# Near bias of the second softmax of three heads added by the vector engine, outputs of the first attention scaled by the scalar engine

## The chip, the cores and the metric

One core of a Trainium2 chip. The metric is device time in microseconds of one execution, lower is better.

## The reference

One layer of a streaming encoder on x of 1024 frames by 1024 channels: an RMSNorm, one projection, two mixers side by side, gates, an output projection, a residual and a last RMSNorm. The first mixer is a differential attention with 4 heads; the second is an attention with 8 heads over 256 keys that an indexer selects for each query. The part that matters here is the first one:

```
s = einsum('bqhd,bkhd->bhqk', qb, k) * scale + bias     # T5 bias by relative position
s = where(allowed, s, -inf)                             # key chunk <= query chunk, chunks of 64
p = softmax(q1, k1) - lam * softmax(q2, k2)
ao = einsum('bhqk,bkhd->bqhd', p, v)
```

Its output is normed, scaled and multiplied by a SiLU gate.

## The kernel before

The kernel is written engine by engine, with semaphores that each engine waits on by hand; every engine runs its instructions in the order written. The program has these stages: norm and transposes of x, the indexer's scores, the first projection (groups A), the **first attention** (252 to 381 us), the second projection (groups B), the second attention, the output projection.

Top-k selection runs on the vector engine (`select`: rounds of MAX8 and MATCH_REPLACE8): one part before the first attention, the larger part right after it and beside the second projection. It ends with the mask for the second attention, whose PSUM moves on the scalar engine wait for `mask_made`.

The first attention has 32 steps: 4 heads (blocks 0 to 3) times 8 tiles of 128 queries, in the order 2, 4, 6, 7, 5, 3, 1, 0. Tile i sees 128(i+1) keys, so the widths of a block are 384, 640, 896, 1024, 768, 512, 256, 128. Each step s has two softmaxes (m = 0, 1), and the engines work on it in a pipeline:

- TensorE, `scores(ph, s, m)`: q times k in float32r in two passes, then for the nearest 256 columns the bias. The bias is split in a high and a low part and added by two matmuls with the identity (L1171, L1172). A 640-wide tile has its band in two banks, so it needs two such pairs. Later come `turn` (transposes of the combined probabilities), `fill` (a slice of the next projection) and `weigh` (the product with V, L1208), which run one step behind.
- Vector engine, step s: `finishA(s-2)` (L1517) scales the output of step s-2 out of PSUM by 1/sum; `far_min(0, s+1, 0)` (L1453), the maximum (a minimum of negated scores) of the next first softmax; `invert` (L1482), `factor` (L1498) and `combine` (L1507), which subtracts the second softmax from the first; `far_min(0, s+1, 1)`.
- Scalar engine, step s: `turned(s-1)` (L872) copies the turned probabilities to SBUF, `exp(s+1, 0)` (L861), `finish(s-2)` squares the scaled output and sums it, `exp(s+1, 1)`.
- GpSimd gates the scaled output (L647), once for each step, and between those splits q and k of the next head into float32r parts (`split_q`, `split_k`). The split for head b+1 starts with step 8b-2. Two DMA copies of the split keys follow (`copy_keys`), for which the first scores of that head wait.

In the second attention the vector engine already adds the bias itself: `far_min` on the far columns and `soften` (L1474), a custom instruction that adds the bias to the scores in PSUM and takes the minimum in one pass; it is followed by a read of its accumulator.

Of the kernel before, what the change touches and what calls it, by code (L numbers as in the profile page):

```python
# [22 lines left out]
P = 128  # L23
CHUNK = 64
# [17 lines left out]
MASKED = 1e30  # L42
# [30 lines left out]
def build(nc, x, norm_w, w_in, w_out, lambda_q1, lambda_k1, lambda_q2, lambda_k2, subln_w,  # L73
# [61 lines left out]
    biasA_hi, _ = place("biasA_hi", [P, A_HEADS, BAND], f32r)  # L135
    biasA_lo, _ = place("biasA_lo", [P, A_HEADS, BAND], f32r, at=bias_at)
    ident_r, _ = place("ident_r", [P, P], f32r)
    k1_low = [place(f"k1_zero_low{b}", [P, SEQ], f32r)[0] for b in range(2)]
# [46 lines left out]
    with ctx:  # L185
# [7 lines left out]
        def bank(n):  # L193
            return psum[:, n * HALF:(n + 1) * HALF]
# [143 lines left out]
        def quads_through(ph, s):  # L338
            return quads[ph, s][-1][0] + 1
# [58 lines left out]
        def same_slot(n):  # L398
# [3 lines left out]
            return max(k for k in range(n) if k % SW == n % SW and k not in FILLS)  # L402

        def units_before(ph, b):

            return 2 * (ph * STEPS + b * TILES)
# [7 lines left out]
        def _(sp):  # L414
# [52 lines left out]

            def load_bias(h):
                sp.dma_start(bias[:, h, :],
                             bass.AP(scratch, h * RELS + P - 1, [[nh * RELS - 1, P], [1, BAND]])  # L470
                             ).then_inc(bias_loaded, 16)
# [9 lines left out]
            for h in range(A_HEADS):  # L481
                load_bias(h)
            for n in range(DB + SW, Q0 - 2):
                load_chunk(n)
# [221 lines left out]
        def _(act):  # L706
# [168 lines left out]
            def finish(s):  # L875

                if s >= 1:
                    act.wait_ge(o_squared, s)
                act.wait_ge(o_moved, s + 1)
                act.activation(sq_junk[:, :], o_tmp[:, s % 4, :], ACT.Square,  # L880
                               accum_out=ssA[:, s:s + 1]).then_inc(o_squared, 1)
# [3 lines left out]
            for s in range(STEPS + 2):  # L885
                qs = quads[0, s - 1] if 1 <= s <= STEPS else []
                turned(0, qs)
                if s + 1 < STEPS:
                    exp(0, s + 1, 0)
                if s >= 2:  # L890
                    finish(s - 2)
                if s >= 1 and s % TILES == 0:
                    move_fill(s // TILES - 1)
                if s + 1 < STEPS:
                    exp(0, s + 1, 1)
                if s == 13:
                    high(Q0 + 2)
                elif s == 17:
                    high(Q0 + 3)
                elif s == STEPS - 1:  # L900
                    high(Q0 + 4)
# [43 lines left out]
        def _(pe):  # L945
# [193 lines left out]
            def scores(ph, s, m):  # L1139
# [22 lines left out]
                for c in range(0, length, HALF):  # L1162
# [3 lines left out]
                    near = max(c, length - BAND)  # L1166
                    banded = (masked or ph == 0) and near < c + w
                    ins = pe.matmul(o, q[:, qt], low[:, c:c + w], start=False, stop=not banded)  # L1168
# [106 lines left out]
        def _(dve):  # L1275
# [144 lines left out]

            dve.wait_ge(bias_loaded, 16 * A_HEADS)
            dve.memset(bias[0:CHUNK, 0:A_HEADS, BAND - CHUNK:BAND], MASKED).then_inc(bias_masked, 1)


# [21 lines left out]
            def far_min(ph, s, m):  # L1446
# [4 lines left out]
                dve.wait_ge(s_ready, u + 1)  # L1451
                if ph == 0:
                    dve.tensor_reduce(negmax[:, u % 4:u % 4 + 1], score_of(u, 0, P * (i + 1)), AX.X, ALU.min  # L1453
# [8 lines left out]
            def soften(ph, s, m):  # L1462
# [7 lines left out]
                if u in far_done:  # L1470
                    dve.wait_ge(dve_own, far_done[u])
                    least = farmin[:, u % 4:u % 4 + 1]
                o = score_of(u, length - w, length)
                dve.tensor_tensor_reduce(out=o, in0=o, in1=bias[:, h, BAND - w:BAND], scale=1.0,  # L1474
                                         scalar=least, op0=ALU.add, op1=ALU.min,
                                         accum_out=negmax[:, u % 4:u % 4 + 1]).then_inc(max_ready, 1)

            def invert(ph, s):

                c = 2 * s % 8  # L1480
                dve.wait_ge(exp_done, 2 * (ph * STEPS + s) + 2)
                inverted[ph, s] = later(dve.reciprocal(rinv[:, c:c + 2], rsum[:, c:c + 2]))  # L1482
# [27 lines left out]

            def finishA(s):

                dve.wait_ge(pv_done, quads_through(0, s))
                if s >= 4:
                    dve.wait_ge(o_gated, s - 3)
                    dve.wait_ge(o_squared, s - 3)
                dve.tensor_scalar(o_tmp[:, s % 4, :], bank(O_BANK)[:, 0:P],  # L1517
                                  rinv[:, 2 * s % 8:2 * s % 8 + 1], None, ALU.mult).then_inc(o_moved, 1)

            ROUNDS = TOPK // 8  # L1520
# [5 lines left out]
            far_min(0, 0, 0)  # L1526
            far_min(0, 0, 1)
            for s in range(STEPS):
                if s >= 2:
                    finishA(s - 2)  # L1530
                if s + 1 < STEPS:
                    far_min(0, s + 1, 0)
                invert(0, s)
                factor(s)
                combine(s)
                if s + 1 < STEPS:
                    far_min(0, s + 1, 1)
            finishA(STEPS - 2)
            finishA(STEPS - 1)
            select(1, SEL0 + 1)  # L1540
# [5 lines left out]
            inverse_root(rA, ssA, rstdA, iw[:, 0:STEPS])  # L1546
            dve.wait_ge(bias_loaded, 16 * nh)
            link(dve.memset(bias[0:CHUNK, A_HEADS:nh, BAND - CHUNK:BAND], MASKED))
# [104 lines left out]
```

## Time and profile before

| what | value |
|---|---|
| median of 3 runs | 789.06 us (788.75 to 790.1) |
| profiled execution | 789.29 us, its span 787.4 us |
| PE busy | 753.8 us (96%) |
| PEld busy | 631.1 us (80%) |
| DVE busy | 613.3 us (78%) |
| ACT busy | 304.6 us (39%) |
| POOL busy | 318.8 us (40%) |
| granted TensorE clock | 0.997 |

PE is TensorE, DVE the vector engine, ACT the scalar engine, POOL is GpSimd. The durations of matmuls overlap, since they are pipelined: the step from one start to the next tells what one costs. The same holds to a smaller degree for the vector and the scalar engine, where a start lies up to 0.1 us ahead of the end before it when nothing is waited for.

### The profile page before, as it was taken

How to read it: one execution, taken by the hardware profiler on the slowest of the kernel's cores; microseconds unless marked ns; L12 is line 12 of the kernel's file. 1: busy time of each engine (PE TensorE's matmuls, PEld its weight loads, DVE VectorE, ACT ScalarE, POOL GpSimd, SP SyncE). 2: the span in 40 equal slices, each digit the busy share in tenths (PEclk: the TensorE clock that was granted, in tenths of full speed). 3: DMA queues.
4: the chain of work that ended last, by engine and by line, in shares of the span. 5: the costliest groups of instructions: out<-in, count | busy, mean ns of one | idle time of the engine just before them, and what ended most of it. 6: DMA issues, size and time to landing. Idle time of an engine off the chain costs nothing.

```text
span 787.4 us, 11733 instructions
## 1 busy us (share of the span) xinstructions
PE 753.8 (96%) x4161; PEld 631.1 (80%) x4161; DVE 613.3 (78%) x1300; ACT 304.6 (39%) x677; POOL 318.8 (40%) x383
## 2 busy tenths in 40 slices
PE   3999999999999999999999999998999999899996
PEld 2765888888887888889888888887888888788885
DVE  3738999999999979978899999994767667524343
ACT  5437222130315566757421313007545455422221
POOL 5320121223538857751355554457996400300000
PEclk9999999999999999999999999999999999999999
DMA  7242111111210011040121111300311100222231
GB/s 261 73 122 67 41 41 53 46 49 54 68 54 0 1 41 29 14 122 1 41 63 45 54 43 51 81 1 27 109 54 55 28 2 1 70 79 79 81 107 53
DMA packets 24560, 44.54 MB, mean 57 GB/s; under 512 B 3076, under 2 KB 9912, under 8 KB 24376
## 3 DMA queue, kind: packets, MB, share of 16 engines
q1 hardware_dynamic: 24504, 43.81, 18.6%
q8 instruction: 33, 0.54, 0.3%
q14 instruction: 23, 0.19, 0.1%
HBM read 35.40 MB, written 6.57 MB: 53 GB/s over the span
## 4 chain that ended last, share of the span: by engine, by line
PE 70%; DVE 23%; ACT 3%; issue 2%; DMA 1%; POOL 1%; SPq 0%; DVEq 0%; ACTq 0%; POOLq 0%
PE psum L1103 22%; PE psum L1208 11%; PE psum L1269 11%; DVE score L1434 9%; DVE top L1429 9%; PE psum L1190 5%; PE psum L1165 4%; PE psum L1003 4%; PE psum L1168 4%; PE psum L1031 3%; PE psum L1047 2%; ACT probsT_B L872 1%; DVE small L1453 1%; PE psum L1176 1%; DVE probs L1507 1%
## 5 line engine op out<-in xcount | busy, mean ns | idle before, releaser
L560 POOL TENSOR_TENSOR w_lo<-w_raw,w_hi 128x512 fp32r<-128x512 f32 x60 | 77.8, 1300 | 219.3 <-ACT w_hi L715 218.9
L1434 DVE MATCH_REPLACE8 score<-top,score 128x768 f32<-128x768 f32 (+5 forms) x176 | 157.3, 907 | 0.0
L1429 DVE MAX8 top<-score 128x8 f32<-128x768 f32 (+5 forms) x176 | 148.2, 909 | 1.0
L715 ACT ACTIVATE w_hi<-w_raw 128x512 fp32r<-128x512 f32 x60 | 37.7, 630 | 215.0 <-PE psum L1103 209.2
L861 ACT ACTIVATE probs<-psum,small 128x384 f32<-128x384 f32 (+7 forms) x128 | 94.8, 741 | 49.0 <-DVE small L1453 32.2
L1103 PE MATMUL psum<-w_hi,big_hi 128*128 128x512 f32 x256 | 99.6, 389 | 0.0
L1103 PE MATMUL psum<-w_lo,big_hi 128*128 128x512 f32 x256 | 99.6, 389 | 0.0
L1103 PE MATMUL psum<-w_hi,big_lo 128*128 128x512 f32 x256 | 99.6, 389 | 0.0
L1208 PE MATMUL psum<-v,probsT_B 128*128 128x64 f32 x576 | 74.8, 274 | 3.7 <-ACT probsT_B L872 2.6
L1208 PEld LDWEIGHTS psum<-v,probsT_B 128*128 128x128 f32 x576 | 70.4, 192 | 8.0 <-ACT probsT_B L872 3.6
L1103 PE MATMUL psum<-big_hi,w_hi 128*128 128x512 f32 x192 | 74.9, 390 | 0.0
L1103 PE MATMUL psum<-big_lo,w_hi 128*128 128x512 f32 x192 | 74.7, 389 | 0.0
L1103 PE MATMUL psum<-big_hi,w_lo 128*128 128x512 f32 x192 | 74.7, 389 | 0.0
L1190 PE MATMUL psum<-ident,probs 128*128 128x128 f32 x432 | 63.8, 274 | 1.6 <-issue 1.3
L1103 PEld LDWEIGHTS psum<-w_hi,big_hi 128*128 128x128 f32 x256 | 48.1, 188 | 10.1
L1103 PEld LDWEIGHTS psum<-w_lo,big_hi 128*128 128x128 f32 x256 | 48.1, 188 | 10.0
L1453 DVE TENSOR_REDUCE small<-psum 128x1 f32<-128x384 f32 (+7 forms) x64 | 48.0, 751 | 10.4 <-PE psum L1172 9.6
L1103 PEld LDWEIGHTS psum<-w_hi,big_lo 128*128 128x128 f32 x256 | 48.1, 188 | 9.8
L1190 PEld LDWEIGHTS psum<-ident,probs 128*128 128x128 f32 x432 | 49.7, 145 | 2.3 <-issue 1.5
L1269 PE MATMUL psum<-big_hi,mx_hi 128*128 128x512 f32 x128 | 50.5, 394 | 0.7 <-DVE mx_lo L1601 0.7
L1269 PE MATMUL psum<-big_hi,mx_lo 128*128 128x512 f32 x128 | 49.9, 390 | 0.0
L1269 PE MATMUL psum<-big_lo,mx_hi 128*128 128x512 f32 x128 | 49.8, 389 | 0.0
(172 smaller groups left out, 1567.0 us busy)
## 6 DMA issues: line engine op xcount, KB each, us to landing
w_raw<-in_w_in SPq DMA_DIRECT2D x62, 256.0 KB, 2.6
xs<-in_x SPq DMA_DIRECT2D x8, 512.0 KB, 6.7
k_high_twice<-k_high_twice SPq DMA_DIRECT2D x16, 256.0 KB, 3.7
xres<-in_x SPq DMA_DIRECT2D x8, 512.0 KB, 3.6
out_y<-y_out SPq DMA_DIRECT2D x16, 256.0 KB, 2.1
w_tail<-in_w_out SPq DMA_DIRECT2D x10, 256.0 KB, 2.6
bias_scratch<-bias_row SPq DMA_DIRECT2D x1, 2304.0 KB
bias<-bias_scratch SPq DMA_DIRECT2D x12, 128.0 KB, 3.2
```

The source lines that it names most:

```text
L560: pool.tensor_tensor(lo[:, 0:cols], w_staged(n)[:, 0:cols], hi[:, 0:cols].bitcast(f32), ALU.subtract).then_inc(w_lo_made, 1)
L715: act.activation(w_parts(n)[0][:, 0:cols], w_staged(n)[:, 0:cols], ACT.Copy).then_inc(w_hi_made, 1)
L861: act.activation(probs_of(ph, s, m)[:, 0:length], score_of(u, 0, length), ACT.Exp, bias=negmax[:, u % 4:u % 4 + 1], scale=-1.0, accum_out= ...
L1003: ins = pe.matmul(o, a[:, d, ws], b[:, d, hs], start=(d == 0 and k == 0), stop=(d == DB - 1 and k == 2))
L1103: ins = pe.matmul(o, a, b, start=(d == 0 and k == 0), stop=(d == DB - 1 and k == 2))
L1165: pe.matmul(o, q[:, qt], k[:, c:c + w], start=True, stop=False)
L1190: ins = pe.transpose(bank(T_BANK + q % 2)[:, k * P:(k + 1) * P], p[:, (j + k) * P:(j + k + 1) * P], ident[:, :])
L1208: ins = pe.matmul(o, probsT[ph][:, q % 4, k * P:(k + 1) * P], v[:, j + k, cols], start=(j + k == 0), stop=(j + k == i))
L1269: ins = pe.matmul(o, a[:, t % 2, e, :], w[:, e, cols], start=(e == 0 and k == 0), stop=(e == DB - 1 and k == 2))
L1429: ins = dve.max(top8[:, i - SEL0, :], sc)
L1434: ins = dve.match_replace(sc, top8[:, i - SEL0, :], sc, TAKEN)
L1453: dve.tensor_reduce(negmax[:, u % 4:u % 4 + 1], score_of(u, 0, P * (i + 1)), AX.X, ALU.min).then_inc(max_ready, 1)
```

## The change

For the second softmax (m = 1) of heads 0 to 2 the two bias matmuls are left out. The vector engine takes the minimum of the far columns only, then adds the bias to the nearest 256 columns with `soften`. It reads the bias from a new tile `soft_bias`, filled by three more DMA loads behind the first four of the bias, and masked by a memset of its own. The scaling of the outputs, `finishA` on the vector engine, is gone; the scalar engine does it now (`finish`, an activation with the reciprocal as its scale) at the start of its step, and what was `finish` is called `square_o`. `invert` gets a wait on `o_moved`, for the scaling of four steps before.

```
+        def by_vector(ph, s, m):
+
+            return ph == 0 and m == 1 and place_of(0, s)[0] < SOFT_HEADS
...
+            for h in range(SOFT_HEADS):
+                load_bias(h, soft_bias)
...
             def finish(s):
 
+                act.wait_ge(combined, s + 1)
+                act.wait_ge(pv_done, quads_through(0, s))
+                if s >= 4:
+                    act.wait_ge(o_gated, s - 3)
+                act.activation(o_tmp[:, s % 4, :], bank(O_BANK)[:, 0:P], ACT.Copy,
+                               scale=rinv[:, 2 * s % 8:2 * s % 8 + 1]).then_inc(o_moved, 1)
+
+            def square_o(s):
...
                 qs = quads[0, s - 1] if 1 <= s <= STEPS else []
+                if s >= 2:
+                    finish(s - 2)
                 turned(0, qs)
                 if s + 1 < STEPS:
                     exp(0, s + 1, 0)
                 if s >= 2:
-                    finish(s - 2)
+                    square_o(s - 2)
...
-                    banded = (masked or ph == 0) and near < c + w
+                    banded = (masked or ph == 0 and not by_vector(ph, s, m)) and near < c + w
...
-            dve.wait_ge(bias_loaded, 16 * A_HEADS)
+            dve.wait_ge(bias_loaded, 16 * (A_HEADS + SOFT_HEADS))
             dve.memset(bias[0:CHUNK, 0:A_HEADS, BAND - CHUNK:BAND], MASKED).then_inc(bias_masked, 1)
+            link(dve.memset(soft_bias[0:CHUNK, :, BAND - CHUNK:BAND], MASKED))
...
-                if ph == 0:
+                if by_vector(ph, s, m):
+                    if far:
+                        far_done[u] = later(dve.tensor_reduce(farmin[:, u % 4:u % 4 + 1], score_of(u, 0, far),
+                                                              AX.X, ALU.min))
+                elif ph == 0:
...
             far_min(0, 0, 1)
+            soften(0, 0, 1)
             for s in range(STEPS):
-                if s >= 2:
-                    finishA(s - 2)
                 if s + 1 < STEPS:
                     far_min(0, s + 1, 0)
                 invert(0, s)
...
                 combine(s)
                 if s + 1 < STEPS:
                     far_min(0, s + 1, 1)
-            finishA(STEPS - 2)
-            finishA(STEPS - 1)
+                    if by_vector(0, s + 1, 1):
+                        soften(0, s + 1, 1)
```

The vector engine in block 1, from the combine of the 896-wide tile to that of the 1024-wide one. Before (L1453 reduction, L1517 scaling, L1482 reciprocal, L1498 factor, L1507 combine):

```order
L1507 SCALAR_TENSOR_TENSOR probs<-probs,small 128x896 [waits dve_own]
L1453 TENSOR_REDUCE small<-psum 128x1 [waits s_ready]
L1517 TENSOR_SCALAR o_tmp<-psum,small 128x128 [waits o_squared,o_gated,pv_done]
L1453 TENSOR_REDUCE small<-psum 128x1 [waits s_ready]
L1482 RECIPROCAL small<-small 128x2 [waits exp_done]
L1498 SCALAR_TENSOR_TENSOR small<-small 128x1 [waits dve_own]
L1507 SCALAR_TENSOR_TENSOR probs<-probs,small 128x1024 [waits dve_own]
```

After the change, at the same place (L1474 and L1477 reductions, L1499 the bias add and its accumulator read, L1509 reciprocal, L1525 factor, L1534 combine):

```order
L1534 SCALAR_TENSOR_TENSOR probs<-probs,small 128x896 [waits dve_own]
L1474 TENSOR_REDUCE small<-psum 128x1 [waits s_ready]
L1499 ISA psum,small<-psum,soft_bias,small 128x256 [waits dve_own]
L1499 ISA small 128x1
L1477 TENSOR_REDUCE small<-psum 128x1 [waits s_ready]
L1509 RECIPROCAL small<-small 128x2 [waits exp_done,o_moved]
L1525 SCALAR_TENSOR_TENSOR small<-small 128x1 [waits dve_own]
L1534 SCALAR_TENSOR_TENSOR probs<-probs,small 128x1024 [waits dve_own]
```

The scaling has left its place behind the second softmax's reduction, and the bias add with its read stands there.

The scalar engine in block 1, from the second exponential of the 768-wide tile to that of the 512-wide one. Before (L861 exponential, L872 copy of turned probabilities, L880 square):

```order
L861 ACTIVATE probs,small<-psum,small 128x768 [waits combined,max_ready]
L872 ACTIVATE probsT_A<-psum 128x512 [waits pv_done,t_ready] x2
L861 ACTIVATE probs,small<-psum,small 128x512 [waits t_ready,max_ready]
L880 ACTIVATE sq_junk,small<-o_tmp 128x128 [waits o_moved,o_squared]
L861 ACTIVATE probs,small<-psum,small 128x512 [waits combined,max_ready]
```

After the change (L869 exponential, L889 the scaling, L880 copies, L897 square):

```order
L869 ACTIVATE probs,small<-psum,small 128x768 [waits combined,max_ready]
L889 ACTIVATE o_tmp<-psum,small 128x128 [waits o_gated,pv_done,combined]
L880 ACTIVATE probsT_A<-psum 128x512 [waits pv_done,t_ready] x2
L869 ACTIVATE probs,small<-psum,small 128x512 [waits t_ready,max_ready]
L897 ACTIVATE sq_junk,small<-o_tmp 128x128 [waits o_moved,o_squared]
L869 ACTIVATE probs,small<-psum,small 128x512 [waits combined,max_ready]
```

The scaling stands between the second exponential and the copies that the product with V waits for.

## Rows read from the trace of the kernel before

**Rows 1.** Busy time by stretch (us; x instructions; clock; DMA), blocks 1, 3, selection.
```profile
286.18:318.72 32.54, 31.68 (x218) 28.30 (x218) 29.31 (x49) 20.95 (x62) 23.99 (x30) 1.00 0.10 25
...
351.00:382.00 31.00, 30.58 (x216) 27.91 (x215) 23.13 (x49) 22.22 (x67) 5.12 (x10) 1.00 0.08 25
...
382.00:531.50 149.50, 149.50 (x660) 123.48 (x659) 148.14 (x247) 29.52 (x49) 78.03 (x114) 1.00 0.18 50
```

**Rows 2.** Timeline of the vector engine: start us, duration us, line, operation.
```profile
297.73 1.21 DVE L1453 TENSOR_REDUCE small<-psum 128x1 f32<-128x1024 f32 x1
298.86 0.34 DVE L1517 TENSOR_SCALAR o_tmp<-psum,small 128x128 f32<-128x128 f32 x1
299.12 0.94 DVE L1453 TENSOR_REDUCE small<-psum 128x1 f32<-128x768 f32 x1
...
300.21 0.17 DVE L1482 RECIPROCAL small<-small 128x2 f32<-128x2 f32 x1
...
317.19 0.56 DVE L1453 TENSOR_REDUCE small<-psum 128x1 f32<-128x384 f32 x1 [0.21 <-PE psum L1172]
317.66 0.34 DVE L1517 TENSOR_SCALAR o_tmp<-psum,small 128x128 f32<-128x128 f32 x1
```

**Rows 3.** Timeline of the scalar engine in block 1.
```profile
289.94 0.80 ACT L861 ACTIVATE probs<-psum,small 128x640 f32<-128x640 f32 x1 [1.25 <-DVE small L1453]
...
298.97 1.12 ACT L861 ACTIVATE probs<-psum,small 128x1024 f32<-128x1024 f32 x1 [1.86 <-DVE small L1453]
299.99 0.19 ACT L861 ACTIVATION_READ_ACCUMULATOR probs<-psum,small 128x1 f32 x1
...
309.87 0.86 ACT L872 ACTIVATE probsT_A<-psum 128x512 f32<-128x512 f32 x2
...
317.78 0.58 ACT L861 ACTIVATE probs<-psum,small 128x384 f32<-128x384 f32 x1 [0.52 <-DVE small L1453]
...
318.85 0.28 ACT L872 ACTIVATE probsT_A<-psum 128x128 f32<-128x128 f32 x1 [0.40 <-PE psum L1190]
```

**Rows 4.** Timeline of TensorE in blocks 1 and 2.
```profile
310.61 1.57 PE L1208 MATMUL psum<-v,probsT_A 128*128 128x128 f32 x12
...
321.53 0.28 PE L1171 MATMUL psum<-biasA_hi,ident_r 128*128 128x256 f32 x1
321.64 0.28 PE L1172 MATMUL psum<-biasA_lo,ident_r 128*128 128x256 f32 x1
321.78 0.55 PE L1190 MATMUL psum<-ident,probs 128*128 128x128 f32 x3
```

**Rows 5.** Line 1474, minimum/median/maximum ns; and timeline in the second attention.
```profile
L1474 DVE CUSTOM_DVE_ANT_0 psum<-psum,bias,small x48: 493/493/495, 536.9 to 675.8; 128x256 f32<-128x256 f32 x48
...
564.16 0.49 DVE L1474 CUSTOM_DVE_ANT_0 psum<-psum,bias,small 128x256 f32<-128x256 f32 x1
564.57 0.14 DVE L1474 DVE_READ_ACCUMULATOR2_ANT small<- 128x1 f32 x1
```

**Rows 6.** Timelines of GpSimd, then TensorE, around block 2.
```profile
318.08 0.46 POOL L647 TENSOR_TENSOR mixA<-mixA,o_tmp 128x128 f32<-128x128 f32 x1 [2.08 <-DVE o_tmp L1517]
...
342.79 0.52 POOL L593 MEMSET kT_r<- 64x512 f32 x1
...
347.79 0.41 PE L1165 MATMUL psum<-k_high_twice,qT_r 128*128 128x384 f32 x1 [0.95 <-DMA k_high_twice<-k_high_twice]
```

**Rows 7.** Timelines of the vector engine and GpSimd at 313 us.
```profile
313.01 1.03 DVE L1498 SCALAR_TENSOR_TENSOR small<-small 128x1 f32<-128x1 f32 x1
...
312.75 1.29 POOL L560 TENSOR_TENSOR wf_lo<-w_raw,wf_hi 128x512 fp32r<-128x512 f32 x1 [2.79 <-ACT wf_hi L715]
```

**Rows 8.** Timelines: vector engine, then scalar engine, at the selection's two ends.
```profile
379.24 0.35 DVE L1507 SCALAR_TENSOR_TENSOR probs<-probs,small 128x128 f32<-128x128 f32 x1
...
381.29 4.39 DVE L1429 MAX8 top<-score 128x8 f32<-128x512 f32 x5
...
532.91 4.03 ACT L774 ACTIVATE mixB<-psum 128x512 f32<-128x512 f32 x8
```

More of the change, by code:

```diff
@@ L136, in build @@
     biasA_lo, _ = place("biasA_lo", [P, A_HEADS, BAND], f32r, at=bias_at)
+    SOFT_HEADS = 3
+    soft_bias, _ = place("soft_bias", [P, SOFT_HEADS, BAND], f32)
     ident_r, _ = place("ident_r", [P, P], f32r)
@@ L466, in _, with load_bias @@
             sp.wait_ge(band_stored, 32)
-            def load_bias(h):
-                sp.dma_start(bias[:, h, :],
+            def load_bias(h, into=bias):
+                sp.dma_start(into[:, h, :],
                              bass.AP(scratch, h * RELS + P - 1, [[nh * RELS - 1, P], [1, BAND]])
@@ L1473, in soften @@
                 o = score_of(u, length - w, length)
-                dve.tensor_tensor_reduce(out=o, in0=o, in1=bias[:, h, BAND - w:BAND], scale=1.0,
+                added = (soft_bias if ph == 0 else bias)[:, h, BAND - w:BAND]
+                dve.tensor_tensor_reduce(out=o, in0=o, in1=added, scale=1.0,
                                          scalar=least, op0=ALU.add, op1=ALU.min,
@@ L1480, in invert @@
                 c = 2 * s % 8
+                if ph == 0 and s >= 4:
+                    dve.wait_ge(o_moved, s - 3)
                 dve.wait_ge(exp_done, 2 * (ph * STEPS + s) + 2)
@@ L1508, in combine @@
                                          op0=ALU.mult, op1=ALU.add).then_inc(combined, 1)
[L1511 to L1518, printed above, removed]
             ROUNDS = TOPK // 8
@@ L1546, in _ @@
             inverse_root(rA, ssA, rstdA, iw[:, 0:STEPS])
-            dve.wait_ge(bias_loaded, 16 * nh)
+            dve.wait_ge(bias_loaded, 16 * (nh + SOFT_HEADS))
             link(dve.memset(bias[0:CHUNK, A_HEADS:nh, BAND - CHUNK:BAND], MASKED))
```

## Prediction

> **What bounds the kernel now.** I read the busy time by stretch first. The first attention runs from 252.4 to about 381 us in four blocks of eight steps, one block for each head. In block 1 (286.18 to 318.72, 32.54 us) TensorE is busy 31.68 and the vector engine 29.31: both nearly full, so neither number alone says who sets the pace. In block 3 (351 to 382) TensorE has 30.58 of 31.00 and the vector engine only 23.13; there TensorE sets it. From 382 to 531.5 the vector engine is full with the top-k selection (148.14 of 149.50), TensorE with the second projections [rows 1].
>
> Then the rows of the vector engine in the middle of block 1. For a tile of 1024 keys it runs reduction, scaling of the output, the next step's first reduction, reciprocal, with starts 297.73, 298.86, 299.12, 300.21 and no hole, while the same engine near 317 has room [rows 2]. So a block has two halves. With the large tiles (640, 896, 1024, 768) a loop sets the pace: second softmax's reduction, its exponential on the scalar engine, reciprocal, factor, combine, next second reduction. With the small ones (512 down to 128, and 384 after them) TensorE does, and the vector engine waits for it. A saving counts only in the half where its engine leads.
>
> Last, two places outside. The keys of the last head come from a chain on GpSimd that starts at 318.08, right behind the gating of step 14, runs without a pause to 343.3 (its last memset starts at 342.79), and after two copies by DMA lets TensorE start block 3 at 347.79 after a wait of 0.95 [rows 6]. And the selection starts at 381.29, after the last scaling of the outputs, though the last combine started at 379.24 and took 0.35. The selection's end releases the scalar engine, which moves eight banks (532.91, 4.03 us) [rows 8].
>
> **The change, part by part.**
>
> TensorE loses one pair of bias matmuls for each of 24 second softmaxes, and one more for each of the three tiles of 640, whose band crosses a bank: 27 pairs. The pair's rows say 0.28 each, but the starts are 321.53, 321.64 and, for what follows, 321.78, so a pair costs 0.25 [rows 4]. That is 27 x 0.25 = 6.8 us of TensorE, 2.25 a block, if TensorE always led.
>
> The vector engine gets a bias add for each. Its price: 0.493 us, 48 times alike; start to its accumulator read 0.41, and the read 0.14 [rows 5]. It replaces the nearest 256 columns of a reduction, which I price by 1024 against 768 columns: 1.21 - 0.94 = 0.27 [rows 2]. From start to the maximum being ready a 1024 tile goes from 1.21 to 0.94 + 0.03 + 0.41 + 0.14 = 1.52 (0.03 is the step from an end to what waits for it, as from 300.18 to 300.21 [rows 2, 3]), so +0.31; the same for all tiles with a far part. Tiles of 256 and 128 have none; their add is about 0.06 longer than the reduction (estimate).
>
> It loses the scaling, 0.26 from start to start (298.86 to 299.12) [rows 2]. How much of it the loop gets back depends on what the reciprocal waits for. Behind the 1024 tile the exponential starts at 298.97, its accumulator read at 299.99 lasts 0.19, and the reciprocal starts at 300.21: it waits for the exponential, so the saving is 0 there. A 640 tile's exponential is 0.80 against 1.12, and the next reduction is longer than it, so the 0.26 comes back; for 896 I put 0.17 [rows 2, 3]. Over the four large tiles of a block: 4 x 0.31 - 0.26 - 0.17 = +0.8 us, a loss, because this half follows the loop and not the sum of busy time (the vector engine's sum falls).
>
> The scalar engine gets the scaling. The trace has no such row; the nearest are its copy of 128x128 out of PSUM, 0.28, and below, 0.26 start to start of the vector engine's own; I take 0.28 [rows 2, 3]. What matters is what is queued behind it: it stands after the second exponential and before the copies of the turned probabilities (309.87, two in 0.86). TensorE's product with V in that step starts at 310.61, just when the first of those copies can be done, so it waits on this already [rows 3, 4]. After the change: +0.8 from the large tiles, +0.31 from the 512 tile's own bias add, +0.28 from the scaling, about +1.4. From there TensorE leads and drops two pairs before the next head, -0.5. Block 1 as a whole: +0.9 to +1.0, taken as +1.0. Block 0 enters with nothing late and TensorE is ahead in more of it; I take 0 as an estimate, between -2.25 (all pairs count) and +1.0 (as block 1).
>
> Block 2 ends in the wait for the keys, and here something else becomes late. The output of step 14 is scaled now at 317.66, right behind a reduction that starts at 317.19; GpSimd goes on at 318.08 [rows 2, 6]. After the change it is scaled behind the exponential of step 16: reduction ended at 317.75, +1.0 of block 1, +0.4 for a bias add on a 384 tile less what comes earlier (estimate), exponential and read 0.7 (0.58 busy and its accumulator), then 0.28: 320.1 instead of 318.0, +2.1 [rows 3]. The chain is the same work, so block 3 starts at 347.79 + 2.1. Block 2's own TensorE work would be about 1.4 late by then (1.0 from block 1 and some 0.4 of its own), of which the wait of 0.95 absorbs all but 0.4 [rows 6]; the keys are later and decide. Block 3 has no edit that TensorE feels; +2.1 is handed through.
>
> After it the two last scalings no longer stand before the selection: it starts at 379.24 + 0.35 = 379.6 plus the shift, 1.7 earlier than 381.29. TensorE's projections lose 0 of this: they end 2.1 later, but the scalar engine's moves wait for the selection now and have about 2 us to give [rows 8].
>
> The three extra bias loads (issued at about 62 us) and a memset of 64 rows lie before the selection's first rounds; I cost them at nothing. If a load were late, the vector engine would start its rounds late; its slack before the first attention is under 1 us (estimate).
>
> **Sum:** 2.1 - 1.7 = +0.4. The profiled execution took 789.29, the median is 789.06, 0.23 lower; on the median 789.5.
>
> **A rule against the trace.** The factor, one element per partition, normally takes 0.2 us; at 313.01 it took 1.03 and ended at 314.04, the end of GpSimd's subtraction (312.75, 1.29) [rows 7]. So a part of the loop in blocks 0 to 2 is waiting for GpSimd, and I take it as unchanged. The Trainium skill, SBUF — State Buffer, section "Who interferes with whom", says that a vector instruction with two SBUF inputs is blocked for the whole of a GpSimd instruction that reads SBUF, and one with a single SBUF input is not. By that the new bias add (one input in PSUM) pays nothing, and the 48 equal durations [rows 5] agree; were it blocked like the factor, 24 times up to 1.29 - 0.03, the loop would grow by up to 30 us. By the same rule only the alignment of factor and combine changes, and a single alignment can be worth about 0.8 (1.03 - 0.22).
>
> **Rivals.**
> (1) TensorE sets the pace nearly everywhere. For it: 31.68 of 32.54 busy. Against: the vector engine's rows without a hole. Then blocks 0 and 1 give 2 x 2.25 = -4.5, the keys' chain starts 4.5 earlier but 1.1 later for being behind the exponential: block 3 at -3.4, with the tail -5.1: 784.0. Chance 0.17.
> (2) Slower: the loop of factor and combine meets GpSimd more often. GpSimd's chain is one unbroken run through the large tiles, and a longer loop leaves more of its steps inside it. It decides once two or more extra stalls of 0.8 fall in blocks 0 to 2 ahead of the keys, or the chain itself is stretched as much; three are +2.4: 791.9. For it: the stall at 313.01. Against: the chain's length is fixed and the stalls have both signs. Chance 0.30.
> (3) The keys do not decide (GpSimd gets step 14 in time): block 3 at +0.4, with the tail -1.3: 787.8. Chance 0.15.
> My forecast, the balance above, 789.5 with its own range 788.3 to 790.8: chance 0.38.
>
> **How the numbers follow.** Change can be told from none beyond 0.2%, 1.6 us: 787.5 and 790.6. Faster: rival 1 and a third of rival 3 and a little of the forecast, 0.25. Slower: most of rival 2 and the forecast's edge, 0.32. Same: 0.43. The range leaves out most of rival 1 and the far end of rival 2: 785.0 to 792.4.
>
> **What would show it.** In the changed profile: pairs of second-softmax bias gone in blocks 0 to 2; the bias add at 0.49 also while GpSimd works; the reciprocal waiting for the exponential in nearly every large tile; the V product waiting for copies by the scalar engine; block 3's start 2 us late with a wait for the keys; the selection's first row 1.7 earlier relative to it. I am wrong if block 1 is shorter than 32.5 us, or if block 3 starts before 347.

## Result: 0.28% slower, and the profile after

The changed kernel takes 791.67 us (median of 6 runs, 789.74 to 792.27), the kernel before in the same session 789.0 (788.38 to 790.48). The ratio is 1.0028, 95% interval 1.0018 to 1.0038: 2.2 us slower. The profiled execution took 792.27 us, span 790.5, at the same granted clock of 0.997; that of before took 789.29.

The page of the changed kernel gives each engine's busy time (us, share of the span, instructions), and the windows give it for three stretches that are close to blocks 0, 1 and 2 (columns as in [rows 1]):

```profile
PE 749.8 (95%) x4107; PEld 624.5 (79%) x4107; DVE 613.4 (78%) x1311; ACT 312.2 (39%) x709; POOL 318.4 (40%) x383
```

```profile
252.40:286.00 33.60, 29.76 (x197) 26.04 (x196) 28.15 (x57) 22.67 (x65) 21.85 (x26) 1.00 0.11 25
286.00:319.00 33.00, 29.71 (x194) 25.60 (x193) 28.39 (x53) 22.08 (x67) 23.97 (x29) 1.00 0.10 24
319.00:352.00 33.00, 28.94 (x187) 24.43 (x186) 28.48 (x51) 21.58 (x67) 23.52 (x28) 1.00 0.07 18
```

TensorE was busy 31.68 of 32.54 us in block 1 [rows 1]. Now it is busy 29.71 of 33.00 there and 28.94 of 33.00 in block 2: it stands idle for three to four microseconds of a block. Its busy time over the kernel fell by 4 us (753.8 to 749.8), and the time went up. What it waits for in the attention, before (252 to 382 us) and then after (252 to 385), in total us, times, longest:

```profile
PE psum L1165 <- ACT probs L861: 3.1, 7, 1.0
PE psum L1165 <- DMA k_high_twice<-k_high_twice: 0.9, 1, 0.9
```

```profile
PE psum L1184 <- ACT probs L869: 5.9, 7, 1.2
PE psum L1227 <- ACT probsT_A L880: 3.7, 7, 0.8
PE psum L1209 <- DVE probs L1534: 1.3, 3, 0.7
```

These are the exponentials, the copies of the turned probabilities and the combine; the wait for the keys is gone. The vector engine's total did not fall (613.3 to 613.4). That is the first thing to see, since the change takes the scaling away from it.

Cut at the start of the combine of the 128-wide tile of each block, at the first scores and at the selection, the two profiled executions differ so:

| stretch | before | after | difference |
|---|---|---|---|
| start to the first scores | 251.57 | 251.83 | +0.26 |
| first scores to last combine of block 0 | 32.51 | 33.35 | +0.84 |
| block 1 | 32.54 | 33.79 | +1.25 |
| block 2 | 32.95 | 35.03 | +2.08 |
| block 3 | 29.67 | 29.34 | -0.33 |
| last combine to selection | 2.05 | 0.27 | -1.78 |
| selection to the scalar engine's start behind the mask | 150.32 | 151.14 | +0.82 |
| the rest | 257.68 | 257.52 | -0.16 |

The sum is +2.98 us. The loss is in blocks 0 to 2, +4.2, half of it in block 2; the tail gives back 1.8 and loses half of that again at the end of the selection.

**Block 1, vector engine and GpSimd.** The timeline after, as in [rows 2]: start, duration, line. L1509 is the reciprocal, L1525 the factor, L1534 the combine, L575 GpSimd's subtractions in the splits of the next head's k.

```profile
302.51 0.17 DVE L1509 RECIPROCAL small<-small 128x2 f32<-128x2 f32 x1 [0.53 <-ACT probs L869]
302.71 0.22 DVE L1525 SCALAR_TENSOR_TENSOR small<-small 128x1 f32<-128x1 f32 x1
302.97 2.25 DVE L1534 SCALAR_TENSOR_TENSOR probs<-probs,small 128x1024 f32<-128x1024 f32 x1
...
305.85 0.49 DVE L1499 CUSTOM_DVE_ANT_0 psum<-psum,soft_bias,small 128x256 f32<-128x256 f32 x1
...
307.54 0.17 DVE L1509 RECIPROCAL small<-small 128x2 f32<-128x2 f32 x1 [0.59 <-ACT probs L869]
307.74 0.58 DVE L1525 SCALAR_TENSOR_TENSOR small<-small 128x1 f32<-128x1 f32 x1
308.35 2.11 DVE L1534 SCALAR_TENSOR_TENSOR probs<-probs,small 128x768 f32<-128x768 f32 x1
...
302.86 1.27 POOL L575 TENSOR_TENSOR kT_r<-kT,k_high_twice 64x512 fp32r<-64x512 f32 x1
...
307.02 1.28 POOL L575 TENSOR_TENSOR k_zero_low<-kT,k_high_twice 64x512 fp32r<-64x512 f32 x1
308.38 1.26 POOL L575 TENSOR_TENSOR kT_r<-kT,k_high_twice 64x512 fp32r<-64x512 f32 x1
```

Two things stand here. The reciprocal now waits 0.53 and 0.59 for the exponential in the tiles of 1024 and 768, where before the hole in front of it was 0.15 and 0.20: the 0.26 of the removed scaling is spent in waiting there. And the combines of 1024 and 768 take 2.25 and 2.11. Undisturbed they take 1.28 and 1.02 (rows of an experiment below). Each begins within 0.11 us of the start of a GpSimd subtraction of 1.26 or 1.27 and pays 0.97 and 1.09. The factor at 307.74 ends at 308.32, when the subtraction of 307.02 does (308.30). The bias add between them takes 0.49, as all 18 of this form in the attention do (0.491 to 0.494), whatever GpSimd does.

**Block 2.** Before, and then after, the same rows of the vector engine (factor and combine of the tiles 896 to 768):

```profile
327.99 0.74 DVE L1498 SCALAR_TENSOR_TENSOR small<-small 128x1 f32<-128x1 f32 x1
328.76 1.59 DVE L1507 SCALAR_TENSOR_TENSOR probs<-probs,small 128x896 f32<-128x896 f32 x1
...
332.96 0.35 DVE L1498 SCALAR_TENSOR_TENSOR small<-small 128x1 f32<-128x1 f32 x1
333.34 2.40 DVE L1507 SCALAR_TENSOR_TENSOR probs<-probs,small 128x1024 f32<-128x1024 f32 x1
...
337.88 0.22 DVE L1498 SCALAR_TENSOR_TENSOR small<-small 128x1 f32<-128x1 f32 x1
338.13 1.38 DVE L1507 SCALAR_TENSOR_TENSOR probs<-probs,small 128x768 f32<-128x768 f32 x1
```

```profile
330.69 1.19 DVE L1525 SCALAR_TENSOR_TENSOR small<-small 128x1 f32<-128x1 f32 x1
331.91 1.59 DVE L1534 SCALAR_TENSOR_TENSOR probs<-probs,small 128x896 f32<-128x896 f32 x1
...
336.50 1.34 DVE L1525 SCALAR_TENSOR_TENSOR small<-small 128x1 f32<-128x1 f32 x1
337.87 2.38 DVE L1534 SCALAR_TENSOR_TENSOR probs<-probs,small 128x1024 f32<-128x1024 f32 x1
...
342.77 0.57 DVE L1525 SCALAR_TENSOR_TENSOR small<-small 128x1 f32<-128x1 f32 x1
343.38 2.11 DVE L1534 SCALAR_TENSOR_TENSOR probs<-probs,small 128x768 f32<-128x768 f32 x1
...
336.54 1.28 POOL L575 TENSOR_TENSOR k_zero_low<-kT,k_high_twice 64x512 fp32r<-64x512 f32 x1
337.90 1.27 POOL L575 TENSOR_TENSOR kT_r<-kT,k_high_twice 64x512 fp32r<-64x512 f32 x1
...
344.73 0.52 POOL L601 MEMSET kT_r<- 64x512 f32 x1
```

The factor moves one element per partition. For the tile of 1024 it takes 1.34 (0.35 before), and the combine behind it is hit again by the next subtraction. In these three tiles factor and combine pay 2.5 us more than before. I call the excess of these two over their undisturbed durations (factor 0.22; combines of 384 to 128 wide, in the order of a block, 0.62, 0.89, 1.15, 1.28, 1.02, 0.75, 0.48, 0.35) the stall. Summed over a block (blocks 0, 1, 2) it is 4.09, 6.87, 5.22 before and 4.97, 7.10, 7.22 after. The excess need not come back one to one as time: what it costs depends on what the other engines wait for.

**The keys.** TensorE at the start of block 3, as in [rows 6]:

```profile
351.32 1.13 PE L1227 MATMUL psum<-v,probsT_A 128*128 128x128 f32 x8
352.21 0.42 PE L1184 MATMUL psum<-k_high_twice,qT_r 128*128 128x384 f32 x1
```

No wait. The chain on GpSimd ends 1.94 later than before (last memset at 344.73 against 342.79 [rows 6]), TensorE comes 4.42 later (352.21 against 347.79). Before, TensorE could start 4.48 us after the end of the last memset (343.31 to 347.79), when the two copies had landed; the same time after the memset's end at 345.25 gives 349.7 (estimate), 2.5 us ahead of TensorE.

**The end of the selection.** The mask's conversions on the vector engine, before and after, and GpSimd beside them:

```profile
526.22 1.03 DVE L1554 TENSOR_SCALAR mask<-score 128x384 bf16<-128x384 f32 x1
527.17 4.36 DVE L1556 TENSOR_SCALAR mask<-score 128x512 bf16<-128x512 f32 x5
```

```profile
528.53 0.36 DVE L1571 TENSOR_SCALAR mask<-score 128x384 bf16<-128x384 f32 x1
528.80 5.87 DVE L1573 TENSOR_SCALAR mask<-score 128x512 bf16<-128x512 f32 x5
...
530.20 1.40 POOL L575 TENSOR_TENSOR q_low_high<-qT,q_low_high 64x512 fp32r<-64x512 f32 x1
...
532.58 1.54 POOL L575 TENSOR_TENSOR qT_r<-qT,q_part 64x512 fp32r<-64x512 f32 x1
```

Six conversions take 5.39 together before and 6.23 after. They overlap six of GpSimd's instructions that split q for the second attention where it was four, and those are stretched too (1.54, where the same instruction takes 1.28 elsewhere).

### The profile page after: what moved, and what is told of

The parts are those of the page before. It is cut to its first block, busy times and chain, and to the rows that moved or that the text cites. A ratio compares the mean times of both kernels' runs of the same rounds, so it can differ in the third digit from the quotient of the medians.

```text
span 790.5 us, 11703 instructions
## 1 busy us (share of the span) xinstructions
PE 749.8 (95%) x4107; PEld 624.5 (79%) x4107; DVE 613.4 (78%) x1311; ACT 312.2 (39%) x709; POOL 318.4 (40%) x383
## 4 chain that ended last, share of the span: by engine, by line
PE 66%; DVE 27%; ACT 3%; issue 2%; DMA 1%; SPq 0%; DVEq 0%; ACTq 0%
PE psum L1122 22%; PE psum L1227 11%; PE psum L1288 11%; DVE score L1454 9%; DVE top L1449 9%; PE psum L1209 5%; PE psum L1184 4%; PE psum L1187 3%; PE psum L1022 3%; PE psum L1050 3%; DVE probs L1534 2%; PE psum L1066 1%; DVE small L1525 1%; ACT probsT_B L880 1%; PE psum L1195 1%
## 5 line engine op out<-in xcount | busy, mean ns | idle before, releaser
L869 ACT ACTIVATE probs<-psum,small 128x384 f32<-128x384 f32 (+7 forms) x128 | 94.9, 742 | 53.2 <-DVE small L1499 47.2
L1631 DVE TENSOR_TENSOR y<-psum,xres 128x512 f32<-128x512 f32 x16 | 11.1, 691 | 46.8 <-PE psum L1288 46.8
```

What stands on the lines that cost most here:

```text
L869: act.activation(probs_of(ph, s, m)[:, 0:length], score_of(u, 0, length), ACT.Exp, bias=negmax[:, u % 4:u % 4 + 1], scale=-1.0, accum_out= ...
```

## The experiments

Theory A: the scaling sits badly on the scalar engine, in front of the copies that the product with V waits for. Theory B: the vector engine's loop is held by GpSimd, the change makes this worse, and it takes the slack away that hid it. The expectations, written before each run, use letters of their own: A is the theory A above, S is the part of B that blames GpSimd's reads (R is its negation), L holds the vector engine's own longer loop to be the limit, without GpSimd, and P holds TensorE to be. The edits are against the kernel before, unless said otherwise. The table gives, for each profiled execution, the attention (first scores to last combine), its stall in blocks 0, 1 and 2, the way from the last combine to the selection, and from there to the scalar engine's start behind the mask (for e6, where that engine is held longer, to the mask's own end); then the median, that of the kernel before in the same session, and the ratio.

| kernel | attention | stall | to selection | to mask | median (before) | ratio, 95% |
|---|---|---|---|---|---|---|
| before | 127.67 | 4.09, 6.87, 5.22 | 2.05 | 150.32 | 789.0 | |
| after | 131.51 | 4.97, 7.10, 7.22 | 0.27 | 151.14 | 791.67 (789.0) | 1.0028, 1.0018 to 1.0038 |
| e1_scale_only | 129.00 | 5.75, 7.95, 5.04 | 0.27 | 151.62 | 790.09 (789.37) | 1.0011, 1.0003 to 1.0020 |
| e2_bias_only | 127.77 | 3.79, 6.02, 4.35 | 2.05 | 150.37 | 789.51 (789.37) | 1.0001, 0.9992 to 1.0010 |
| e3_pairs_out | 126.19 | 4.50, 6.81, 5.16 | 2.05 | 150.34 | 788.2 (789.37) | 0.9987, 0.9978 to 0.9996 |
| e4_add_only | 128.92 | 3.80, 6.00, 4.36 | 2.05 | 150.33 | 790.83 (789.37) | 1.0023, 1.0013 to 1.0032 |
| e5_before_free | 122.30 | 0, 0.73, 1.15 | 2.05 | 150.37 | 784.04 (790.0) | 0.9932, 0.9915 to 0.9948 |
| e6_after_free | 118.38 | 0.51, 1.21, 0.07 | 0.27 | 151.1 | 778.92 (790.0) | 0.9866, 0.9848 to 0.9884 |
| e7_tail_only | 127.81 | 4.15, 6.92, 5.29 | 0.27 | 151.29 | 788.6 (790.0) | 0.9989, 0.9980 to 0.9998 |
| e8_last_head | 125.60 | 2.95, 6.92, 5.29 | 0.27 | 151.29 | 786.58 (790.0) | 0.9966, 0.9953 to 0.9980 |
| e9_scale_early | 130.63 | 5.32, 5.85, 4.18 | 0.27 | 151.30 | 792.28 (789.0) | 1.0046, 1.0033 to 1.0060 |
| e10_small_tiles | 125.75 | 2.90, 7.22, 5.49 | 0.27 | 151.29 | 786.81 (789.0) | 0.9978, 0.9968 to 0.9988 |
| e11_scale_free | 121.98 | 0.27, 1.01, 1.40 | 0.27 | 151.62 | 783.23 (789.0) | 0.9929, 0.9915 to 0.9943 |
| e12_small_early | 127.49 | 4.25, 7.10, 5.18 | 0.27 | 151.32 | 788.21 (789.0) | 0.9990, 0.9981 to 0.9999 |

The first scores start between 250.5 and 252.8 in these executions, without order, so the columns count from there. Each row is one profiled execution. Between before and e7, between e2 and e4 and between e8 and e10 in block 0 a stall sum repeats to about 0.1. But e8 has the code of e7 in block 0, apart from a bias load and a memset long before the attention, and 2.95 of stall there for 4.15: what happens ahead of the attention can be worth 1.2 us of stall. So a difference of that size in one block is not by itself the work of an edit in that block.

**One part alone: e1, the scaling.** The changed kernel without the bias part:

```
+        def by_vector(ph, s, m):
+
+            return False
```

> Only the scaling moves to the scalar engine; the bias stays on TensorE for every softmax. Theory L (the loop of second reduction, exponential, reciprocal, factor, combine sets the pace in large tiles, and the bias add is what lengthens it): the selection starts 1.7 us earlier behind the last combine, the loop gets back some 0.4 a block, the V product pays 0.28 here and there: 1.5 to 2.5 us faster than before. Theory A (the scaling standing before the copies on the scalar engine is what costs): no gain or up to 2 us slower, with TensorE waiting for the copies in each large tile.

The attention is 1.33 longer, with 2.56 more stall in blocks 0 to 2. So the move of the scaling costs time by itself, although it takes 0.26 a step from the vector engine. That is what A expected, and L, which expected 1.5 to 2.5 us less, was wrong. But A also expected TensorE to wait for the copies in each large tile, and it waits for them twice, 0.4 us in all, too little for 1.33.

**e2, the bias part alone.** `finishA` stays on the vector engine, the scalar engine's `finish` is left out of the changed kernel.

> Only the bias of the second softmax of heads 0 to 2 moves to the vector engine; the scaling stays there too. Theory L: the loop carries both, so 4 to 6 us slower than before. Theory A: about as before, within 1.5 us. Theory P (TensorE sets the pace): 4 us or more faster.

Nothing: +0.10 in the attention, ratio 1.0001. L's 4 to 6 us did not come, nor P's gain; A allowed this (within 1.5 us). The two parts give +1.43 when added, +3.84 together. Most of the rest is in blocks 2 and 3: they take 62.62 before, 62.65 with e1, 62.79 with e2 and 64.37 with both. The stall in block 2 is below that of before in each alone (5.04 and 4.35) and 7.22 with both.

**e3, the pairs alone.** The second softmaxes of three heads get neither bias nor mask from anyone:

```
-                    banded = (masked or ph == 0) and near < c + w
+                    banded = (masked or ph == 0 and not (m == 1 and b < 3)) and near < c + w
```

> The kernel before with the bias matmuls of the second softmax of heads 0 to 2 left out and nothing put in their place, so these softmaxes lack their bias and mask. It measures what the 27 pairs (6.8 us of TensorE) are worth. Theory L: 1 to 2.5 us faster, since they count only in the small tiles and the keys of the last head come from GpSimd. Theory P: 5 us or more faster.

27 pairs give 1.48 us in the attention, 1.0 in the median ratio: a fifth of the 6.8 that they occupy on TensorE.

**e4, the adds alone.** e2 with the bias matmuls left in (the bias is counted twice):

```
-                    banded = (masked or ph == 0 and not by_vector(ph, s, m)) and near < c + w
+                    banded = (masked or ph == 0) and near < c + w
```

> The bias matmuls stay, and the vector engine adds the same bias once more in the second softmax of heads 0 to 2, so it is counted twice there. It measures what the adds cost alone. Theory L: slower than before by the cost of e2_bias_only and the worth of e3_pairs_out together, 6 to 8 us. Theory P: within 1 us of before, since the vector engine has room.

+1.25 in the attention, with 2.0 less stall than before, and a ratio of 1.0023: neither the 6 to 8 us of L nor within the 1 us of P. e3's gain and e4's loss cancel, as e2 shows.

**Without GpSimd's reads: e5 on before, e6 on after.** For heads 1 to 3 of the first attention the splits of q and k are left out, and memsets write their tiles; the scores of these heads are zero plus bias. The same lines in both, here for k:

```
+                if ph == 0 and b > 0:
+                    for t in (k0[0:HEAD, c], k1[HEAD:P, c], k1_low[b % 2][HEAD:P, c], kT_r[0:HEAD, b, c]):
+                        link(pool.memset(t.bitcast(f32), 0.0))
...
+                    return
```

> The kernel before, with GpSimd's splits of q and k for heads 1 to 3 of the first attention replaced by as many memsets of the same tiles, which write only. Left out: the real values of those parts, so heads 1 to 3 see zero scores. Theory S (factor and combine stand in line behind GpSimd instructions that read SBUF, some 5 to 7 us a block): factor and combine at their short durations, blocks 1 and 2 near 30 us instead of 32.5 and 33.0. Theory R (the long factors come from something else): blocks unchanged.

> The changed kernel with the same replacement, heads 1 to 3 see zero scores. Theory S: without the stalls TensorE sets the pace in both kernels, so the change shows its 27 pairs: at least 3 us faster than e5_before_free from the start of the attention to its end. Theory A (the scaling in front of the copies on the scalar engine is the loss): still 1 us or more slower than e5_before_free.

The timeline of e5 in block 1, vector engine and then GpSimd:

```profile
297.03 0.22 DVE L1518 SCALAR_TENSOR_TENSOR small<-small 128x1 f32<-128x1 f32 x1
297.28 1.28 DVE L1527 SCALAR_TENSOR_TENSOR probs<-probs,small 128x1024 f32<-128x1024 f32 x1
...
301.68 1.02 DVE L1527 SCALAR_TENSOR_TENSOR probs<-probs,small 128x768 f32<-128x768 f32 x1
...
297.47 0.52 POOL L601 MEMSET k_zero_low<- 64x512 f32 x1
298.05 0.52 POOL L601 MEMSET kT_r<- 64x512 f32 x1
```

A GpSimd instruction that only writes disturbs neither factor (0.22) nor combine (1.28, while memsets run). The stall falls from 16.2 us in three blocks to 1.9 (before) and from 19.3 to 1.8 (after). What that is worth differs: 127.67 - 122.30 = 5.4 us in the kernel before, 131.51 - 118.38 = 13.1 us in the changed one. The memsets are also shorter (0.52 each), so GpSimd's chain ends sooner; that can have given at most the 0.9 that TensorE waited for keys before and nothing in the changed kernel, which has no such wait. And the sign of the change turns: e6 is 5.1 us faster than e5 (778.92 against 784.04, same session), while after is 2.2 slower than before. The windows of one stretch in e5 and then e6 say why:

```profile
282.00:312.00 30.00, 30.00 (x215) 28.00 (x215) 23.39 (x47) 20.89 (x61) 15.19 (x29) 1.00 0.10 25
```

```profile
282.00:312.00 30.00, 29.91 (x203) 26.96 (x202) 24.33 (x58) 23.58 (x73) 15.34 (x29) 1.00 0.11 27
```

TensorE is busy 30.00 and 29.91 of 30.00: without stalls it leads in either kernel, the vector engine needs 24 of 30, and what is taken from TensorE counts in part (3.9 us in the attention for 27 pairs of 0.25). In the changed kernel with its stalls it was 29.71 of 33.00.

**e11, the scaling alone, without GpSimd's reads** (e1 with the same memsets).

> e1_scale_only with the splits of heads 1 to 3 replaced by memsets as in e5_before_free (heads 1 to 3 see zero scores). If the 1.3 us that the moved scaling cost the attention in e1_scale_only are a matter of GpSimd: none of it here, attention as in e5_before_free within 0.3 us. If it is the scaling's place in front of the copies: 1 us or more longer than in e5_before_free.

Its attention is 121.98, that of e5 122.30. So the move of the scaling costs nothing where no stall is, and with the 0.4 us of waits for copies in e1 that speaks for B and against A as the price of the move. It does not settle it alone: in e5 and e11 TensorE leads, which could hide a cost of the scaling's place. The bias part can be read off as well, as the difference between two kernels with the scaling moved: with GpSimd's reads it adds 2.5 us to the attention (131.51 against e1's 129.00), without them it takes 3.6 off (e6's 118.38 against 121.98).

**e9, the scaling ahead of the second exponential.** In the changed kernel the scalar engine scales one step earlier, ahead of `exp(s+1, 1)` and not ahead of the copies:

```
-                if s >= 2:
-                    finish(s - 2)
...
+                if 1 <= s <= STEPS:
+                    finish(s - 1)
```

> The changed kernel, with the scaling on the scalar engine taken from behind the second exponential to ahead of it, where that engine waits for the vector engine in large tiles; V products and GpSimd get the output about 1 us earlier. Theory A (what costs is the scaling's place, in the line exponential, scaling, copies, V product, and GpSimd's later start): the attention shrinks by 1.3 us or more against the changed kernel, total 788 to 790. Theory S alone (only the longer loop meets GpSimd): the attention within 0.7 us of the changed kernel, total about 791.5.

Blocks 1 and 2 shrink (33.79 to 32.98, 35.03 to 33.12) and their stall with them (5.85, 4.18). But block 3 takes 30.27 for 29.34 and the first combine to the last of block 0 29.83 for 28.93, so the attention is 0.9 shorter in the profiled execution, between the 1.3 that A expected and the 0.7 that S allowed, and the median is no better: 1.0046 against 1.0028 of the changed kernel, each against its own kernel before. Block 3 of e9, TensorE's product with V, the vector engine's second reduction, and the scalar engine:

```profile
368.49 1.72 PE L1227 MATMUL psum<-v,probsT_A 128*128 128x128 f32 x14
...
368.81 0.95 DVE L1477 TENSOR_REDUCE small<-psum 128x1 f32<-128x768 f32 x1
...
370.30 0.37 ACT L889 ACTIVATE o_tmp<-psum,small 128x128 f32<-128x128 f32 x1 [1.30 <-issue]
370.56 0.89 ACT L869 ACTIVATE probs<-psum,small 128x768 f32<-128x768 f32 x1
```

The maximum for this exponential is there at 369.76. But the scaling stands ahead of it and waits 1.30 for the product with V, which ends at 370.21, so the exponential starts 0.8 late. The tiles of 512, 256 and 128 show the same; in that of 1024 it costs nothing, the exponential (365.75) follows its own maximum there. Of the two places tried, the one behind the exponential delays the copies and the one ahead of it the exponential. That block 0's loss in e9 has the same cause was not tested.

**e7, only the tail.** The last two scalings go to the scalar engine, all others stay:

```
+                if s >= STEPS:
+                    scale_o(s - 2)
...
-            finishA(STEPS - 2)
-            finishA(STEPS - 1)
```

> The kernel before, with only the scalings of the last two steps on the scalar engine. The attention keeps its length, the selection starts 1.8 us earlier. If the mask then meets GpSimd as in e1_scale_only it takes up to 1.3 us longer: 0.5 us faster; if it does not, 1.8 us faster.

The selection starts 1.78 earlier behind the last combine and then takes 151.29 for 150.32: 0.8 net, and the ratio of 0.9989 is 0.9 us (the medians lie 1.4 apart, 788.6 and 790.0). In every kernel without the scalings before the selection this stretch is 151.1 to 151.6; in every other it is 150.3 to 150.4.

**e8, the last head.** The bias add for the second softmax of head 3 alone, and e7's tail:

```
+            return ph == 0 and m == 1 and place_of(0, s)[0] == BLOCKS - 1
```

> The kernel before, with the vector engine adding the bias of the second softmax in the last head only (block 3, where GpSimd is idle and TensorE sets the pace), and the last two scalings on the scalar engine. If the place decides what the pairs are worth: block 3 shrinks by 2 us, with the tail 2.5 to 4 us faster than before. If the loop is the limit there too: only what e7_tail_only gives.

The windows of block 3, before and then e8:

```profile
350.00:378.00 28.00, 28.00 (x202) 26.05 (x202) 21.63 (x43) 19.29 (x57) 3.19 (x7) 1.00 0.13 40
```

```profile
350.00:378.00 28.00, 27.91 (x190) 24.87 (x189) 23.88 (x59) 20.67 (x63) 3.59 (x8) 1.00 0.08 23
```

GpSimd is busy 3 of 28 us and the vector engine has room for the adds. Block 3 takes 28.29 for 29.67: 1.38 of the 2.25 that nine pairs of 0.25 would be (the tile of 640 has two). At 0.9966 this is, with e10, the fastest kernel here that computes the reference: 2.7 us by the ratio, 3.4 between the medians, from the change's own parts put where TensorE leads. But 0.9 us of it is luck: block 0, which e8 does not edit, has 2.95 of stall and is that much shorter between its first and last combine, an alignment that nobody aimed at.

**e10 and e12, more of it.** e10 is e8 with the add for the tiles up to 384 wide of heads 1 and 2 as well; e12 is e10 with every scaling on the scalar engine, placed as in e9.

```
+            return ph == 0 and m == 1 and (place_of(0, s)[0] == 3 or place_of(0, s)[0] > 0 and place_of(0, s)[1] <= SEL0)
```

> As e8_last_head, and the vector engine adds the bias of the second softmax also in the tiles 384, 256 and 128 wide of heads 1 and 2, where TensorE leads. If the place decides: six more pairs, up to 1.5 us less than e8_last_head, of which the keys of the last head can take back the half: 785 to 786. If the adds lengthen the loop there too: as e8_last_head or up to 1 us slower.

> e10_small_tiles with all scalings on the scalar engine, ahead of the second exponential. If that place is free of cost, up to 1 us faster than e10_small_tiles, since the loop gets back 0.2 to 0.4 a block; otherwise equal or slower.

e10 gives nothing beyond e8 (0.9978 and 0.9966, the intervals overlap): six more pairs, 1.5 us of TensorE, make block 1 0.12 shorter and block 2 0.27 longer (33.38 for 33.11, stall 5.49 for 5.29). e12 is worse than e10, 788.21 against 786.81, so the place ahead of the exponential is not free of cost.

## Why the prediction came out as it did

The time, 791.67, lies in the range (785.0 to 792.4) at its upper part. The likeliest case, 789.5, was 2.2 low, and its path was not the one that decided: its sign came out right by luck. The case that held is rival 2, at a chance of 0.30, which gave 791.9. That its number is so close is luck too: it has the end of the attention 4.5 late and the tail at -1.7; the profile has 4.1, and -1.1 for all behind the attention, and the two misses nearly cancel.

- **A pair costs 0.25, 6.8 in all, where TensorE leads.** Where TensorE leads it was worth less, about 0.15 with the add that replaces it: e6 against e5 is -3.9 in the attention for 27 pairs, e8 -1.38 for nine. The view that it counts for little elsewhere held: e3 gives 1.5 for all 27.
- **The bias add, +0.31 a tile, and not held by GpSimd.** It takes 0.49 beside GpSimd in every block. The Trainium skill, SBUF — State Buffer, "Who interferes with whom", which exempts an instruction with one SBUF input outside the two-port modes, agrees. As a price of the loop it was too high: 4 x 0.31 a block is 3.7 in three, and e4, which has the adds alone, is 1.25 longer, though with 2.0 less stall.
- **The scaling on the scalar engine.** I took 0.28 from start to start; it is 0.25 (below), its busy time 0.36. TensorE now waits for the copies behind it before the product with V:

```profile
307.33 0.36 ACT L889 ACTIVATE o_tmp<-psum,small 128x128 f32<-128x128 f32 x1
307.58 1.08 ACT L880 ACTIVATE probsT_A<-psum 128x512 f32<-128x512 f32 x2
...
308.32 0.91 PE L1227 MATMUL psum<-v,probsT_A 128*128 128x128 f32 x6 [0.48 <-ACT probsT_A L880]
```

  There are seven such waits, 3.7 us in all, in the changed kernel, 0.4 in e1 and 1.1 in e2. So it is not the scaling alone that makes them: TensorE without its pair comes to the product earlier, and what it saves there is spent in this wait.

- **Block 1: +1.0.** Measured +1.25. **Block 0: 0.** Measured +0.84, near the bound of +1.0 that I had for it; this was an estimate without a row, and taken like block 1 it would have been nearer.
- **Block 2: the keys decide, block 3 starts at 347.79 + 2.1.** This is the step that failed. The chain moved nearly as forecast (+1.94), but TensorE came at +4.42 and waited for nothing. I had block 2's own lateness at "some 0.4"; it is +2.08 as measured between the combines of 128, while its stall grew by 2.0. Rival 3 said that the keys would not decide, and was right in this and wrong in its time, because it kept the stalls.
- **"I take it as unchanged"**, of the waiting for GpSimd. It was not: 16.2 us became 19.3. Rival 2 named the mechanism, its place and about its size (three extra stalls of 0.8, +2.4).
- **Balance of stalls as a matter of alignment alone.** The price of a stall changed too, and the prediction does not have that. Before, 14.3 us of removed stall were worth 5.4: a good part hid behind TensorE. After, 17.5 were worth 13.1. With the scaling moved but TensorE's work unchanged (e1 against e11) 16.1 were worth 7.0, so most of the rise came with the bias part, which takes work from TensorE and puts it on the vector engine; which of the two does it no run tells.
- **The tail: -1.7.** Measured -1.78. That the gain is kept was wrong: +0.82 comes back at the mask, where the conversions meet GpSimd's splits for the second attention. The same section of the Trainium skill says that a vector engine's `tensor_scalar` can contend with GpSimd in its two-port modes; the rows with 4.36 and 5.87 for the same five instructions agree that it contends; in which mode they ran no row shows. I had looked only at the selection's start.
- **What would show it:** of the six signs four came: pairs gone, 0.49, the wait for copies, the selection 1.7 earlier. The reciprocal's wait came in half: 0.27 to 0.59 in the tiles of 1024 and 768 of blocks 0 to 2, under 0.1 in those of 640 and 896. Block 3 started late, but by 4.4 us and without a wait for the keys.

Shown by runs: that GpSimd's reads turn this change from a gain into a loss (e5 and e6, with e1 and e11 for the parts), and that each part alone costs at most 1.3 in the attention (e1, e2). Not shown: why just both parts together put three tiles of block 2 onto GpSimd's subtractions. The rows show that they meet, not which earlier microsecond decided it, and no run shifted one engine by a known amount against the other.

## What to carry over

A sum of busy time says nothing where an engine waits inside its own instructions: compare each instruction's duration with its shortest one in the trace, and take that excess as a cost that moves when anything in the loop moves. Relief for an engine counts in the stretch where that engine leads and its neighbours are quiet; the same bias add was worth 1.4 us in the one block with a nearly idle GpSimd (e8) and nothing in the three others (e2). And follow a freed start to its end: 1.78 us gained ahead of the selection were 0.96 after it.

## What was unexpected in the hardware

- A tiny instruction waits for the rest of GpSimd's: the factor on 128x1 takes 0.22 alone, 0.58 where it meets the end of a subtraction, and 1.34 beside a whole one that began 0.04 later by the trace (336.50 and 336.54). A combine pays up to 1.12 for one subtraction of 1.28.
- It works both ways. In the attention, GpSimd's subtraction that starts at 334.74 in the kernel before, while a combine is running, takes 2.14 for 1.28, so the chain that makes the keys is stretched too. In the mask's conversions, 128x384 from float32 to bfloat16 takes 0.36 in one kernel and 1.03 in the other, and GpSimd's subtraction beside them 1.54 for 1.28. The durations of single records are therefore no price list unless the other engine is known to be idle.
